# Gathered rows fetched whole, or cut in two at partition 32 or at partition 96, in turn by slot

## The chip, the core and the metric

The kernel runs on one core of one Trainium2 chip. The core has a matrix engine (TensorE, "PE"), a vector engine (VectorE, "DVE"), a scalar engine (ScalarE, "ACT"), a general one (GpSimd, "POOL") and an engine that issues transfers (SyncE, "SP"). Sixteen DMA engines move data between the chip's memory and the core's on-chip memory, which has 128 partitions. The metric is the time on the device, in microseconds, of one launch. Lower is better.

## The reference

One decoder layer over 256 tokens of width 2048, in float32. An input projection feeds a convolution branch and a sparse attention branch, an output projection and a layer norm follow, and then the part that matters here, a lookup of single-neuron experts:

```python
s = einsum('nhcd,hckd->nhck', q, sub_keys)            # 8 heads, 2 key sets of 128 keys
s1, i1 = top_k(s[:, :, 0], 16); s2, i2 = top_k(s[:, :, 1], 16)
cand_i = i1 * 128 + i2                                # 16 x 16 candidates a head
top_s, pos = top_k(s1 + s2, 16)
experts = take_along_axis(cand_i, pos)                # (256, 8, 16), of 16384
h = gelu(einsum('td,thed->the', x, u_tab[experts]))
y = einsum('the,thed->td', softmax(top_s) * h, v_tab[experts])
x = layer_norm(alpha * x + y)
```

Each token needs 128 rows of `u_tab` and the same 128 rows of `v_tab`, 8 KB each. The host puts a row of both next to each other, in one row of 16 KB of `uv_tab`.

## The kernel before

The first 430 us hold the projections, the convolution, the attention and the first layer norm. After them comes a loop over 256 slots. The tokens stand in the 128 partitions, in two tiles (i = 0 and 1) of 128 tokens; slot s stands for tile i and for the j-th expert (of 128) of every token in it, `(i, j) = ROW_OF[s]`. Slots 0 to 49 are of tile 0, then the tiles take turns.

For one slot, POOL issues a gather at L465: an indirect DMA that reads for each of the 128 partitions the row of `uv_tab` whose number stands in that partition of one column of `eid`, and writes it to one of the buffers `uv_row` (128 x 4096 float32, 2 MB; six of them, seven from slot 54 on, `PLACES` and `WIDER_AT`). VectorE then forms the dot product of the first half of each row with the token (`dot`, L1642), ScalarE makes the weight of it (`gelu`, L1158 and L1162) and a diagonal matrix (L1166), TensorE adds the weighted second half of the row to the sum in PSUM (`add_row`, L805), and VectorE adds its last 512 columns up to slot 239 (`add_last`, L1651). A gather into a buffer waits until both additions from the buffer are done (`y_done`, `y_last_done`). POOL takes the slots strictly in order.

Some rows are not fetched. VectorE counts which first keys are wanted most (`popularity`) and chooses sixteen (`choose`, at slot 37); the experts of these keys are computed for all tokens with dense products (`dense_part`, `v_dense`: their blocks come over SP's queue, 1 MB each). `mark` (L1577 to L1590) writes for each block of 16 experts their numbers into `eid`, and adds 16384 to those of the chosen keys: such a number is out of bounds, and the gather moves nothing for that partition. `mark` runs for the 13 of 16 blocks that are not in `BEFORE`, and its last instruction tells POOL by `picked` that the numbers are there. Every slot from 48 on has such blocks. The last two slots (`TAIL`) are gathered in halves, from `last_id`.

Two earlier transfers of POOL are used for comparison below. L425 reads `dist_row` from 16 partitions that lie 8 apart (0, 8, ..., 120) and writes 2 MB to `turned_rows` in the chip's memory, in pieces of 1 KB; L430 then reads these 2 MB back, in the same pieces, into all 128 partitions of `bias`.

`u_in[k]` is the semaphore of buffer k on which the gathers land, 16 for each gather; `dot` waits for 16 times the number of gathers into its buffer so far (`USES`).

Of the kernel before, what the change touches and what calls it, by code (L numbers as in the profile page):

```python
# [7 lines left out]
I32 = mybir.dt.int32  # L8
# [3 lines left out]
ALU = mybir.AluOpType  # L12
ACT = mybir.ActivationFunctionType
AX = mybir.AxisListType

P = 128
D = 2048
S = 256
TI = S // P
# [11 lines left out]
TOP = 16  # L31
SLOTS = PH * TOP
# [19 lines left out]
ALL = TI * SLOTS  # L52
WIDER_AT = 54
PLACE = [s % PLACES if s < WIDER_AT else (s - WIDER_AT + PLACES) % (PLACES + 1) for s in range(ALL)]
USES = [PLACE[:s + 1].count(PLACE[s]) for s in range(ALL)]
BEFORE_IT = [max((r for r in range(s) if PLACE[r] == PLACE[s]), default=-1) for s in range(ALL)]
TAIL = 2
# [9 lines left out]
SKIP = PK * PK  # L67
# [9 lines left out]
ROW_OF = ([(0, j) for j in range(ALONE)] + [((n + 1) % 2, n // 2 + (n % 2) * ALONE) for n in range(2 * (SLOTS - ALONE))]  # L77
          + [(1, j) for j in range(SLOTS - ALONE, SLOTS)])
# [6 lines left out]
BEFORE = [(0, 0), (0, 1), (0, 2)]  # L85
# [10 lines left out]
ASKED = [(0, 0), (0, 1), (1, 1), (1, 0)]  # L96
TURNED = ((0, 2, 1, 3), (0, 1, 2, 3))

def layer(nc, xT, x_tok, w_stream, w_kw, w_sub, conv_p, cln, bucket1h, rel_bias,
          b_out, ln1_col, ln_rows, uv_tab, dense_u, out):
    with ExitStack() as ctx:
        def sb(name, shape, dt=F32):
            return ctx.enter_context(nc.sbuf_tensor(name, shape, dt))

        def sem(name):
            return ctx.enter_context(nc.semaphore(name))
# [10 lines left out]
        def span(i):  # L119

            return slice(0, S) if i else slice(S, S + P)
# [9 lines left out]
        def put(name, where, shape, dt=F32, plus=0):  # L131
            return nc.alloc_sbuf_tensor_at(name, shape, dt, offset=arena0 + (spot[where] + plus) * KB)[:]
# [35 lines left out]
        row = [put(f"uv_row{k}", w, [P, 2 * D], plus=o) for k, (w, o) in enumerate(places)]  # L168
# [59 lines left out]
        val, idxf, posf = ([sb(f"{n}{c}", [P, TOP]) for c in range(2)] for n in ("val", "idxf", "posf"))  # L228
        of_dense = sb("of_dense", [P, TOP])
# [10 lines left out]
        eid = sb("eid", [P, TI * SLOTS], I32)  # L240

        dots = sb("dots", [P, TI * SLOTS])
        gel = sb("gel", [P, TI * SLOTS])
        weight = sb("weight", [P, TI * SLOTS])
        last_f = sb("last_f", [P, TAIL])
        last_id = sb("last_id", [P, 2, TAIL], I32)
# [11 lines left out]
        def at_early(name, shape, offset, dt=F32):  # L258
            return nc.alloc_sbuf_tensor_at(name, shape, dt, offset=early0 + offset)
# [11 lines left out]
        row_gate = at_early("row_gate", [P, TI, SLOTS], 6144)  # L271
# [48 lines left out]
        gate_sub, gate_exp, picked = sem("gate_sub"), sem("gate_exp"), sem("picked")  # L320
# [8 lines left out]
        gates_done, weight_done, y_last_done = sem("gates_done"), sem("weight_done"), sem("y_last_done")  # L329
# [4 lines left out]
        u_in = [sem(f"u_in{k}") for k in range(PLACES + 1)]  # L334
        v_in = [sem(f"v_in{k}") for k in range(TAIL)]
        dots_done, gelu_done, diag_done, y_done = (sem(n) for n in ("dots_done", "gelu_done", "diag_done", "y_done"))
# [66 lines left out]
        def _(pool):  # L403
# [31 lines left out]
            for c in range(2, CC):  # L435
                pool.wait_ge(conv_done, c + 1)
                pool.wait_ge(total_step, c - 1)
                last = pool.tensor_tensor(conv_total, conv_total, convT[:, c, :], ALU.add)
                last.then_inc(total_step if c < CC - 1 else conv_summed, 1)
            pool.wait_ge(squared, 1)  # L440
            for step, n in enumerate((CC // 2, CC // 4, CC // 8)):
                if step:
                    pool.wait_ge(sq_step, step)
                last = pool.tensor_tensor(sq[:, 0:n, :], sq[:, 0:n, :], sq[:, n:2 * n, :], ALU.add)
# [18 lines left out]
            def gather(dst, tab, ids, land):  # L463

                pool.indirect_dma_start(dst, None, tab, bass.IndirectOffsetOnAxis(ap=ids, axis=0),  # L465
                                        bounds_check=tab.shape[0] - 1, oob_is_err=False).then_inc(land, 16)

            halves = uv_tab.rearrange("n (a d) -> (n a) d", a=2)
            for s in range(ALL):
                k = PLACE[s]  # L470
                i, j = ROW_OF[s]
                if j % TOP == 0:
                    pool.wait_ge(picked, ORDER.index((i, j // TOP)) + 1)
                if k == 4 and s < PLACES:
                    pool.wait_ge(q_done, ASKED.index((1, 1)) + 1)
                if k == 5 and s < PLACES:
                    pool.wait_ge(x1_done, TI)
                if s == WIDER_AT:
                    pool.wait_ge(unit_scored, LATER)
                if BEFORE_IT[s] >= 0:  # L480
                    pool.wait_ge(y_done, BEFORE_IT[s] + 1)
                    pool.wait_ge(y_last_done, min(BEFORE_IT[s] + 1, JOIN_AT))
                if s < ALL - TAIL:
                    gather(row[k], uv_tab, eid[:, i * SLOTS + j:i * SLOTS + j + 1], u_in[k])
                else:
                    j = s - (ALL - TAIL)
                    gather(row[k][:, 0:D], halves, last_id[:, 0, j:j + 1], u_in[k])
# [454 lines left out]
        def _(act):  # L942
# [211 lines left out]
            def gelu(s):  # L1154

                i, j = ROW_OF[s]
                act.wait_ge(dots_done, s + 1)
                act.activation(gel[:, s:s + 1], dots[:, s:s + 1], ACT.Gelu).then_inc(gelu_done, 1)  # L1158
                if j % TOP == 0:
                    act.wait_ge(gates_done, ORDER.index((i, j // TOP)) + 1)  # L1160
                act.wait_ge(gelu_done, s + 1)
                act.activation(weight[:, s:s + 1], gel[:, s:s + 1], ACT.Identity, scale=row_gate[:, i, j:j + 1]).then_inc(weight_done, 1)  # L1162
                act.wait_ge(weight_done, s + 1)
                if BEFORE_IT[s] >= 0:
                    act.wait_ge(y_done, BEFORE_IT[s] + 1)
                act.activation(diag[PLACE[s]], ident[:, :], ACT.Identity, scale=weight[:, s:s + 1]).then_inc(diag_done, 1)  # L1166
# [40 lines left out]
            for s in range(3, ALL):  # L1207
# [5 lines left out]
                r, t = s // PACE + 1, s % PACE  # L1213
# [15 lines left out]
        def _(dve):  # L1229
            steps = [0]  # L1230

            def link(ins):

                steps[0] += 1
                ins.then_inc(dve_step, 1)
                dve.wait_ge(dve_step, steps[0])
# [51 lines left out]
            for u in range(CC):  # L1288
                lower(u + 2)
                dve.wait_ge(relu_done, 2 + u + 1)  # L1290
                for j in range(2):
                    for i in range(TI):
                        h = i * NH + 2 * u + j
                        last = dve.scalar_tensor_tensor(out=acc[i][:, :], in0=rel[u % 2][:, j, span(i)], scalar=widx[:, h:h + 1],
                                                        in1=acc[i][:, :], op0=ALU.mult, op1=ALU.add)
# [93 lines left out]
            for hp in range(CC):  # L1389
                for j in range(2):  # L1390
# [4 lines left out]
                    if hp == CC - 2 and j == 0:  # L1395
                        dve.wait_ge(mean_done, 1)
                        for c in range(CC):
                            last = dve.tensor_tensor(convT[:, c, :], convT[:, c, :], ps[7][:, 0:S], ALU.subtract)
# [38 lines left out]
            for n in range(3):  # L1437
# [3 lines left out]
                if n == 0:  # L1441
                    dve.wait_ge(row_in, 16)
                    dve.wait_ge(b_in, 16)
                    for i in range(TI):
                        last = dve.scalar_tensor_tensor(out=x1[:, i, :], in0=x1[:, i, :], scalar=ALPHA, in1=b_all,
                                                        op0=ALU.mult, op1=ALU.add)
# [11 lines left out]
                for i in range(TI):  # L1458
                    last = dve.bn_stats(stats[:, 4 * i + n, :], x1[:, i, n * 512:(n + 1) * 512])
# [65 lines left out]
            def across(t):  # L1525

                return t.rearrange("p (r o) -> p r o", o=1).to_broadcast(square)
# [49 lines left out]
            def mark(i, h):  # L1577

                q = i * PH + h
                first, second = (t[:, i, h * TOP:(h + 1) * TOP] for t in key_of)  # L1580
                dve.scalar_tensor_tensor(out=posf[0][:, :], in0=first, scalar=float(PK), in1=second, op0=ALU.mult, op1=ALU.add)
                link(dve.tensor_tensor(hit[0], across(first), down(dense_key[:, :]), ALU.is_equal))
                link(dve.tensor_reduce(of_dense[:, :], hit[0], AX.X, ALU.add))
                if q == TI * PH - 1:
                    link(dve.scalar_tensor_tensor(out=last_f[:, :], in0=of_dense[:, TOP - TAIL:TOP], scalar=float(SKIP),
                                                  in1=posf[0][:, TOP - TAIL:TOP], op0=ALU.mult, op1=ALU.add))
                    for a in range(2):
                        link(dve.tensor_scalar(last_id[:, a, :], last_f[:, :], 2.0, float(a), ALU.mult, ALU.add))
                dve.scalar_tensor_tensor(out=eid[:, q * TOP:(q + 1) * TOP], in0=of_dense[:, :], scalar=float(SKIP),
                                         in1=posf[0][:, :], op0=ALU.mult, op1=ALU.add).then_inc(picked, 1)  # L1590

            def divide(i, h):

# [40 lines left out]
            def dot(s):  # L1634

                k = PLACE[s]
                dve.wait_ge(u_in[k], 16 * USES[s])
                if s == PLACES:
                    dve.wait_ge(key_copied, len(ASKED))
                if s > PLACES:  # L1640
                    dve.wait_ge(dots_done, s)
                dve.tensor_tensor_reduce(row[k][:, 0:D] if s < PLACES else product, row[k][:, 0:D], x1[:, ROW_OF[s][0], :], 1.0, 0.0, ALU.mult, ALU.add,  # L1642
                                         dots[:, s:s + 1]).then_inc(dots_done, 1)
# [68 lines left out]
            for s in range(ALL - TAIL):  # L1712
# [7 lines left out]
                r, t = s // PACE + 1, s % PACE  # L1720
# [63 lines left out]
            for s in range(ALL - TAIL, ALL):  # L1784
                dve.wait_ge(weight_done, s + 1)
                dve.wait_ge(v_in[s - (ALL - TAIL)], 16)
                for n in range(TAIL_BANKS, 4):
                    last = dve.scalar_tensor_tensor(out=bank(1, n), in0=row[PLACE[s]][:, D + n * 512:D + (n + 1) * 512],
                                                    scalar=weight[:, s:s + 1], in1=bank(1, n), op0=ALU.mult, op1=ALU.add)
# [78 lines left out]
```

## Time and profile before

| | us |
|---|---|
| median of 3 runs | 1663.65 (1663.07 to 1663.74) |
| the profiled execution | 1665.44 |
| its span, from the first to the last instruction | 1663.6 |

| engine | busy us | share of the span |
|---|---|---|
| TensorE, matmul | 1545.1 | 93% |
| VectorE | 1342.8 | 81% |
| ScalarE | 496.2 | 30% |
| GpSimd | 483.5 | 29% |

The DMA engines moved 571.57 MB, 450.03 MB of it over the queue that POOL issues to (q0). A TensorE that is busy 93% is not at its peak for 93%: the profile counts a matmul as busy while it is in the pipeline. The span falls into stages, and a share over all of it says little about any of them. The rows below are therefore mostly of windows, in us from the start of the span. A DMA share is the mean busy share of the 16 DMA engines; a waiting time stands for an engine that is idle until something releases it.

### The profile page before, as it was taken

To read this page: it belongs to the slowest core of one execution; us is meant where nothing else is said; L and a number is where in the kernel's file an instruction comes from. 1 tells how busy PE (TensorE), PEld (TensorE's weight loads), DVE (VectorE), ACT (ScalarE), POOL (GpSimd) and SP (SyncE) were. 2 spreads that over 40 slices of the span, in tenths; PEclk is the share of its full clock that TensorE was granted. 3 is DMA by queue.
4 is the path that set the end of the run, shared out by engine and by line. 5 is a ranking of instruction groups with operands and counts; after the bars stand their busy time and mean duration, and the time that the engine had idled before them with its cause. 6 is when DMAs were issued, how large, how long until landed. Compare 5 with 4: busy or idle time off the path is not lost.

```text
span 1663.6 us, 18502 instructions
## 1 busy us (share of the span) xinstructions
PE 1545.1 (93%) x6332; PEld 993.6 (60%) x6332; DVE 1342.8 (81%) x2260; ACT 496.2 (30%) x1142; POOL 483.5 (29%) x293
## 2 busy tenths in 40 slices
PE   9999999999999888998899999899999999998896
PEld 8999899888765444555455555355555444433332
DVE  4689999766778787988899999899998766655577
ACT  5433344734222221233222222212222311111121
POOL 0100110100123223434444444444544322332231
PEclk9999999999999999999999999999999999999999
DMA  6664544474799999999999999999999999999994
GB/s 248 197 234 177 201 155 151 180 301 177 292 416 426 427 427 428 427 418 399 413 388 404 407 376 405 416 412 380 403 381 401 361 408 416 418 407 382 351 349 183
DMA packets 58669, 571.57 MB, mean 344 GB/s; under 512 B 12969, under 2 KB 13641, under 8 KB 16713
## 3 DMA queue, kind: packets, MB, share of 16 engines
q0 software_dynamic: 39328, 450.03, 66.4%
q1 hardware_dynamic: 18580, 120.22, 19.1%
q8 instruction: 47, 0.77, 0.2%
q14 instruction: 42, 0.34, 0.1%
q10 hardware_dynamic: 672, 0.21, 0.1%
HBM read 665.68 MB, written 4.19 MB: 403 GB/s over the span
## 4 chain that ended last, share of the span: by engine, by line
DMA 39%; PE 38%; DVE 13%; issue 6%; ACT 2%; POOL 1%; SPq 0%; POOLq 0%; DVEq 0%
DMA uv_row<-in_uv_tab,eid 37%; PE psum L805 10%; PE psum L500 6%; PE psum L502 6%; PE psum L501 6%; DVE scratch L1642 5%; PE psum L898 4%; POOL uv_row L465 1%; DMA w_raw<-in_w_stream 1%; PE psum L826 1%; DVE y_last L1651 1%; PE psum L746 1%; DVE first_key L1662 1%; PE psum L630 1%; DVE w_lo L1261 1%
## 5 line engine op out<-in xcount | busy, mean ns | idle before, releaser
L805 PE MATMUL psum<-uv_row,scratch 128*128 128x512 f32 x1560 | 742.0, 614 | 95.1 <-ACT scratch L1166 94.3
L1642 DVE CUSTOM_DVE_ANT_0 scratch<-uv_row,x 128x2048 bf16<-128x2048 f32 x250 | 572.5, 2290 | 206.0 <-DMA uv_row<-in_uv_tab,eid 205.0
L465 POOL DMA_INDIRECT uv_row<-in_uv_tab,eid x254 | 440.4, 1734 | 752.1 <-DVE y_last L1651 402.2
L805 PEld LDWEIGHTS psum<-uv_row,scratch 128*128 128x128 f32 x1560 | 289.8, 193 | 436.8 <-issue 282.2
L1158 ACT ACTIVATE gel<-dots 128x1 f32<-128x1 f32 x256 | 51.9, 203 | 820.9 <-DVE dots L1642 820.8
L500 PE MATMUL psum<-xT_hi,w_hi 128*128 128x256 f32 x640 | 183.8, 287 | 3.5 <-DVE w_lo L1261 2.9
L1651 DVE SCALAR_TENSOR_TENSOR y_last<-uv_row,weight,y_last 128x512 f32<-128x512 f32 x240 | 179.8, 749 | 3.3 <-ACT weight L1162 1.3
L502 PE MATMUL psum<-xT_hi,w_lo 128*128 128x256 f32 x640 | 181.7, 284 | 0.0
L501 PE MATMUL psum<-xT_lo,w_hi 128*128 128x256 f32 x640 | 181.7, 284 | 0.0
L1261 DVE TENSOR_TENSOR w_lo<-w_raw,w_hi 128x2048 fp32r<-128x2048 f32 x62 | 141.7, 2288 | 29.0 <-ACT w_hi L957 28.1
L957 ACT ACTIVATE w_hi<-w_raw 128x2048 fp32r<-128x2048 f32 x62 | 118.8, 1916 | 85.9 <-DMA w_raw<-in_w_stream 85.9
L500 PEld LDWEIGHTS psum<-xT_hi,w_hi 128*128 128x128 f32 x640 | 123.4, 193 | 7.4 <-issue 3.1
L501 PEld LDWEIGHTS psum<-xT_lo,w_hi 128*128 128x128 f32 x640 | 123.5, 193 | 0.1
L502 PEld LDWEIGHTS psum<-xT_hi,w_lo 128*128 128x128 f32 x640 | 123.4, 193 | 0.0
L858 PEld LDWEIGHTS psum<-x1T,dense_unit 128*128 128x128 f32 x512 | 97.4, 190 | 40.6 <-issue 30.7
L898 PE MATMUL psum<-dense_unit,scratch 128*128 128x512 f32 x256 | 121.0, 595 | 0.0
L858 PE MATMUL psum<-x1T,dense_unit 128*128 128x256 f32 x512 | 121.0, 379 | 0.0
L1166 ACT ACTIVATE scratch<-ident,weight 128x128 f32<-128x128 f32 x256 | 102.9, 402 | 8.4
L898 PEld LDWEIGHTS psum<-dense_unit,scratch 128*128 128x128 f32 x256 | 48.8, 192 | 63.4 <-issue 63.4
L1333 DVE SCALAR_TENSOR_TENSOR scratch<-glu_sb,conv_sb,scratch 128x256 f32<-128x256 f32 x203 | 82.7, 478 | 0.0
L886 PEld LDWEIGHTS psum<-scratch,first_key 128*128 128x128 f32 x512 | 65.6, 194 | 24.3 <-issue 24.3
L1162 ACT ACTIVATE weight<-gel,row_gate 128x1 f32<-128x1 f32 x256 | 75.6, 295 | 14.9 <-DVE gate L1630 5.3
(247 smaller groups left out, 1408.7 us busy)
## 6 DMA issues: line engine op xcount, KB each, us to landing
w_raw<-in_w_stream SPq DMA_DIRECT2D x63, 1024.0 KB, 4.8
dense_unit<-in_dense_u SPq DMA_DIRECT2D x16, 1024.0 KB, 11.1
dense_unit<-in_uv_tab SPq DMA_DIRECT2D x16, 1024.0 KB, 11.2
wq_first<-in_w_stream SPq DMA_DIRECT2D x8, 1024.0 KB, 11.4
wq_third<-in_w_stream SPq DMA_DIRECT2D x4, 1024.0 KB, 11.7
uv_row<-in_uv_tab,eid POOLq DMA_INDIRECT x254, 20.9
xT_raw<-in_xT SPq DMA_DIRECT2D x4, 512.0 KB, 5.5
turned_rows<-dist_row POOLq DMA_DIRECT2D x1, 2048.0 KB, 14.0
```

The lines of the kernel that those rows point to most:

```text
L465: pool.indirect_dma_start(dst, None, tab, bass.IndirectOffsetOnAxis(ap=ids, axis=0), bounds_check=tab.shape[0] - 1, oob_is_err=False).then ...
L500: pe.matmul(dst, a[0], b[0], start=first, stop=False)
L501: pe.matmul(dst, a[0], b[1], start=False, stop=False)
L502: return pe.matmul(dst, a[1], b[0], start=False, stop=last)
L805: last = pe.matmul(bank(i, n), diag[k], row[k][:, D + n * 512:D + (n + 1) * 512], start=False, stop=True, skip_group_check=True)
L858: last = pe.matmul(spare[v % 2][:, 0:S], w[:, c, :], x1T[:, c, :], start=c == 0, stop=c == KC - 1)
L898: last = pe.matmul(bank(i, n), mixed[:, v, i * P:(i + 1) * P], dense_unit[v % 2][:, n * 512:(n + 1) * 512], start=v == 0 and n == PE_BANKS ...
L957: act.activation(w_hi[k], w_raw[k], ACT.Copy).then_inc(hi_done, 1)
L1166: act.activation(diag[PLACE[s]], ident[:, :], ACT.Identity, scale=weight[:, s:s + 1]).then_inc(diag_done, 1)
L1261: dve.tensor_tensor(w_lo[k], w_raw[k], w_hi[k].bitcast(F32), ALU.subtract).then_inc(lo_dve, 1)
L1642: dve.tensor_tensor_reduce(row[k][:, 0:D] if s < PLACES else product, row[k][:, 0:D], x1[:, ROW_OF[s][0], :], 1.0, 0.0, ALU.mult, ALU.add, ...
L1651: dve.scalar_tensor_tensor(out=y_last[:, i, :], in0=row[k][:, D + 3 * 512:2 * D], scalar=weight[:, s:s + 1], in1=y_last[:, i, :], op0=ALU. ...
```

## The change

Every gather from slot 49 to slot 253 whose experts are of a block outside `BEFORE` now comes in one of three ways, by its place in the block of 16 (`CUT`): whole; or as two gathers, of partitions 0-31 and 32-127; or as two, of partitions 0-95 and 96-127. Of the 254 whole-row gathers, 65 are cut at 32, 64 at 96, and 125 stay as they are; POOL issues 129 more. The second gather takes its row numbers from `eid_moved`, in which `mark` puts the numbers of the upper partitions at partition 0 and up, with four copies for each block. `dot` waits for the landings of all gathers of its slot (`LANDED`). To make room for `eid_moved`, the buffer `gel` is gone, and the GELU is written over its argument in `dots`.

```diff
+CUTS = (P, 32, 96)
+CUT = [CUTS[ROW_OF[s][1] % TOP % len(CUTS)] if (ROW_OF[s][0], ROW_OF[s][1] // TOP) not in BEFORE and s < ALL - TAIL else P
+       for s in range(ALL)]
+LANDED = [sum(1 + (CUT[r] < P) for r in range(s + 1) if PLACE[r] == PLACE[s]) for s in range(ALL)]
...
-        gel = sb("gel", [P, TI * SLOTS])
+        eid_moved = sb("eid_moved", [P, TI * SLOTS], I32)
...
                 if s < ALL - TAIL:
-                    gather(row[k], uv_tab, eid[:, i * SLOTS + j:i * SLOTS + j + 1], u_in[k])
+                    ids, cut = i * SLOTS + j, CUT[s]
+                    gather(row[k][0:cut], uv_tab, eid[0:cut, ids:ids + 1], u_in[k])
+                    if cut < P:
+                        gather(row[k][cut:P], uv_tab, eid_moved[0:P - cut, ids:ids + 1], u_in[k])
...
-                act.activation(gel[:, s:s + 1], dots[:, s:s + 1], ACT.Gelu).then_inc(gelu_done, 1)
+                act.activation(dots[:, s:s + 1], dots[:, s:s + 1], ACT.Gelu).then_inc(gelu_done, 1)
...
-                dve.scalar_tensor_tensor(out=eid[:, q * TOP:(q + 1) * TOP], in0=of_dense[:, :], scalar=float(SKIP),
-                                         in1=posf[0][:, :], op0=ALU.mult, op1=ALU.add).then_inc(picked, 1)
+                link(dve.scalar_tensor_tensor(out=eid[:, q * TOP:(q + 1) * TOP], in0=of_dense[:, :], scalar=float(SKIP),
+                                              in1=posf[0][:, :], op0=ALU.mult, op1=ALU.add))
+                for n, cut in enumerate(CUTS):
+                    at_cut = slice(q * TOP + n, (q + 1) * TOP, len(CUTS))
+                    for p in range(cut, P, 32):
+                        last = dve.tensor_copy(eid_moved[p - cut:p - cut + 32, at_cut], eid[p:p + 32, at_cut])
+                last.then_inc(picked, 1)
...
-                dve.wait_ge(u_in[k], 16 * USES[s])
+                dve.wait_ge(u_in[k], 16 * LANDED[s])
```

On POOL, the gathers of slots 47 to 53 before (the number in `uv_row1` and so on is the buffer, the shape is partitions x elements):

```order
L465 DMA uv_row5_89<-in_uv_tab,eid 128x4096
L465 DMA uv_row0_84<-in_uv_tab,eid 128x4096
L465 DMA uv_row1_85<-in_uv_tab,eid 128x4096
L465 DMA uv_row2_86<-in_uv_tab,eid 128x4096
L465 DMA uv_row3_87<-in_uv_tab,eid 128x4096
L465 DMA uv_row4_88<-in_uv_tab,eid 128x4096
L465 DMA uv_row5_89<-in_uv_tab,eid 128x4096
```

and the same slots now:

```order
L470 DMA uv_row5_89<-in_uv_tab,eid 128x4096
L470 DMA uv_row0_84<-in_uv_tab,eid 128x4096
L470 DMA uv_row1_85<-in_uv_tab,eid 32x4096
L470 DMA uv_row1_85<-in_uv_tab,eid_moved 96x4096
L470 DMA uv_row2_86<-in_uv_tab,eid 128x4096
L470 DMA uv_row3_87<-in_uv_tab,eid 96x4096
L470 DMA uv_row3_87<-in_uv_tab,eid_moved 32x4096
L470 DMA uv_row4_88<-in_uv_tab,eid 32x4096
L470 DMA uv_row4_88<-in_uv_tab,eid_moved 96x4096
L470 DMA uv_row5_89<-in_uv_tab,eid 128x4096
```

Slots 49, 51 and 52 now have two gathers; no other instruction of POOL has moved. The waits for the buffer stand ahead of the first of the two.

On VectorE, the end of `mark` and the start of `divide` (which sets the gates of the same block) before:

```order
L1583 TENSOR_REDUCE of_dense<-scratch 128x16
L1589 SCALAR_TENSOR_TENSOR eid<-of_dense,posf 128x16
L1595 SCALAR_TENSOR_TENSOR row_gate<-of_dense,gate 128x16
```

and now:

```order
L1591 TENSOR_REDUCE of_dense<-scratch 128x16
L1597 SCALAR_TENSOR_TENSOR eid<-of_dense,posf 128x16
L1602 COPY eid_moved<-eid 32x5 x4
L1608 SCALAR_TENSOR_TENSOR row_gate<-of_dense,gate 128x16
```

Four small copies (32 partitions x 5 numbers each) have come in, and POOL is told only after the last of them. That happens 13 times. TensorE, ScalarE and SyncE have the same instructions in the same order as before.

## Rows read from the trace of the kernel before

**Rows 1.** The page, part 2: DMA in 40 slices of 41.6 us.
```profile
DMA  6664544474799999999999999999999999999994
GB/s 248 197 234 177 201 155 151 180 301 177 292 416 426 427 427 428 427 418 399 413 388 404 407 376 405 416 412 380 403 381 401 361 408 416 418 407 382 351 349 183
```
**Rows 2.** The page, part 4: the chain that ended last, by line.
```profile
DMA uv_row<-in_uv_tab,eid 37%; PE psum L805 10%; PE psum L500 6%; PE psum L502 6%; PE psum L501 6%; DVE scratch L1642 5%; PE psum L898 4%; POOL uv_row L465 1%; DMA w_raw<-in_w_stream 1%; PE psum L826 1%; DVE y_last L1651 1%; PE psum L746 1%; DVE first_key L1662 1%; PE psum L630 1%; DVE w_lo L1261 1%
```
**Rows 3.** Stretches: length, PE, PEld, DVE, ACT, POOL busy (count), PEclk, DMA share, GB/s.
```profile
72.00:75.00 3.00, 3.00 (x27) 3.00 (x27) 2.65 (x6) 1.82 (x1) 0.38 (x2) 1.00 1.00 370
75.00:80.00 5.00, 5.00 (x44) 5.00 (x44) 4.60 (x13) 1.38 (x2) 2.31 (x1) 1.00 0.98 191
88.00:90.00 2.00, 2.00 (x19) 2.00 (x18) 0.43 (x1) 1.47 (x1) 0.00 (x0) 1.00 1.04 360
480.00:700.00 220.00, 191.96 (x621) 114.77 (x620) 176.59 (x384) 56.81 (x160) 67.11 (x42) 0.98 1.01 427
722.00:1066.00 344.00, 314.25 (x958) 179.26 (x957) 311.36 (x647) 98.54 (x268) 153.52 (x77) 0.99 0.98 401
1066.00:1260.00 194.00, 177.66 (x726) 106.23 (x725) 182.65 (x195) 40.54 (x135) 87.40 (x45) 0.95 0.98 397
1270.00:1435.00 165.00, 163.72 (x394) 71.97 (x393) 111.97 (x115) 38.43 (x122) 54.08 (x38) 1.00 0.98 399
1435.00:1566.00 131.00, 120.49 (x267) 50.65 (x266) 77.02 (x78) 23.41 (x78) 37.09 (x27) 0.97 0.97 391
1566.00:1612.00 46.00, 42.24 (x96) 17.52 (x95) 32.60 (x34) 11.87 (x33) 14.43 (x11) 1.00 0.91 345
```
**Rows 4.** VectorE's waits for gathers, 722:1066, 1066:1260, 1435:1566, 1566:1612: us, times, longest.
```profile
DVE scratch L1642 <- DMA uv_row<-in_uv_tab,eid: 25.9, 19, 4.0
...
DVE scratch L1642 <- DMA uv_row<-in_uv_tab,eid: 10.6, 14, 1.8
...
DVE scratch L1642 <- DMA uv_row<-in_uv_tab,eid: 53.9, 25, 4.4
...
DVE scratch L1642 <- DMA uv_row<-in_uv_tab,eid: 14.4, 10, 2.4
```
**Rows 5.** The chain in order of time, 1566 to 1664 us: start, us, what.
```profile
1584.50 22.91 DMA uv_row<-in_uv_tab,eid
...
1618.81 22.25 DMA uv_row<-in_uv_tab,eid
1641.08 2.29 DVE scratch L1642
```
**Rows 6.** The stretch in which the last gathers are under way, columns as in rows 3.
```profile
1620.00:1641.00 21.00, 17.42 (x39) 6.81 (x38) 12.43 (x13) 4.50 (x15) 7.68 (x4) 1.00 0.86 337
```
**Rows 7.** POOL's queue in 722:1066, 1066:1260, 1270:1435, 1435:1566: packets, MB, share.
```profile
q0 software_dynamic: 10682, 120.98, 86.2%
...
q0 software_dynamic: 6658, 76.96, 97.8%
...
q0 software_dynamic: 5342, 58.43, 87.1%
...
q0 software_dynamic: 3938, 43.83, 82.4%
```
**Rows 8.** Line L425: its one instruction, duration ns min/median/max and its start.
```profile
L425 POOL DMA_DIRECT2D turned_rows<-dist_row x1: 1263/1263/1263, 67.6 to 67.6; - x1
```
**Rows 9.** The tile `eid`: duration ns min/median/max; the last line is the gathers' landing.
```profile
L465 POOL DMA_INDIRECT uv_row<-in_uv_tab,eid x254: 987/1740/3047, 431.8 to 1618.8; - x127
L1589 DVE SCALAR_TENSOR_TENSOR eid<-of_dense,posf x13: 174/174/177, 664.2 to 1041.0; 128x16 int32<-128x16 f32 x13
...
DMA to landing us min/median/max: 8.7/20.9/28.7
```
**Rows 10.** A small copy of VectorE, 600 to 1066 us: busy us, mean ns, idle before.
```profile
L1617 DVE COPY gsum<-gate 128x1 f32<-128x1 f32 x12 | 1.8, 147 | 0.0
```
**Rows 11.** The page, part 5: the gathers' issues, busy us, mean ns, idle before.
```profile
L465 POOL DMA_INDIRECT uv_row<-in_uv_tab,eid x254 | 440.4, 1734 | 752.1 <-DVE y_last L1651 402.2
```

More of the change, by code:

```diff
@@ L1161, in gelu @@
                 act.wait_ge(gelu_done, s + 1)
-                act.activation(weight[:, s:s + 1], gel[:, s:s + 1], ACT.Identity, scale=row_gate[:, i, j:j + 1]).then_inc(weight_done, 1)
+                act.activation(weight[:, s:s + 1], dots[:, s:s + 1], ACT.Identity, scale=row_gate[:, i, j:j + 1]).then_inc(weight_done, 1)
                 act.wait_ge(weight_done, s + 1)
```

## The prediction, made before the changed kernel ran

> **What bounds the kernel now.** I read the slices first, then the chain, then windows by stage, then who waits in each. The slices show the DMA engines at 9 tenths from slice 12 on, where the gathers begin, and 427 GB/s at best, then 350 to 420 [rows 1]. The chain that ended last has 37% of the span in gathers, more than any other line [rows 2]. By stage [rows 3]: from 480 to 700 us, before any row is left out, 427 GB/s at a DMA share of 1.01, so 427 is what full engines move. From 722 to 1066 it is 401 GB/s at 0.98 with VectorE busy 311 of 344 us; from 1066 to 1260 397 GB/s, VectorE 183 of 194; from 1270 to 1435 TensorE is busy 163.7 of 165 us and bounds; from 1435 to 1566 nothing computes all the time (TensorE 120 of 131, VectorE 77) and the DMA moves 391. VectorE waits for gathers 25.9, 10.6, 53.9 and 14.4 us in the four windows where TensorE does not bound [rows 4], 105 us together.
>
> Two rows say that the sixteen DMA engines are not loaded alike late in the loop. From 1566 to 1612 us VectorE waits for gathers while the engines are busy only 0.91 of the time and move 345 GB/s [rows 3, 4]. The last whole gather is issued at 1618.81 and takes 22.25 us [rows 5], about 6 times what its bytes need, in a stretch with a DMA share of 0.86 [rows 6]. A gather has landed when its slowest engine is done. Rows of chosen keys are left out, and whoever serves the tokens with few such rows has more to fetch.
>
> **How much a gather moves.** POOL's queue moved 120.98, 76.96, 58.43 and 43.83 MB in the four windows from 722 to 1566 us [rows 7], in which 77, 45, 38 and 27 gathers were issued [rows 3]: 300.2 / 187 = 1.605 MB each. At 427 GB/s that is 3.76 us. The slots come every 344/77 = 4.47, 194/45 = 4.31, 165/38 = 4.34 and 131/27 = 4.85 us, part of which is SP's own loads. So the DMA has next to no slack, and whatever slows a cut gather shows in the end.
>
> **The change, part by part.** POOL: 129 more issues. An issue lasts 0.99 to 3.05 us, 1.74 in the median [rows 9], so 128 to 393 us on an engine that sat idle for 752 us before its gathers [rows 11]. Even two issues of 1.74 fit into a slot of 4.3, so POOL does not bound. The second part of a slot starts one issue later, 1.0 to 3.0 us. Hidden as long as the DMA engines have a backlog, which a landing time of 20.9 us [rows 9] for 3.76 us of bytes shows; if they had none, a buffer comes round every 6 or 7 slots and the price would be 129 x 1.74 / 7 = 32 us. I take 0.
>
> VectorE: 13 x 4 = 52 copies of 32 x 5 numbers. The nearest copy takes 147 ns [rows 10], the instruction ahead of them 174 [rows 9]: 7.6 to 9.0 us in all, in a stage where VectorE idles 33 us of 344 [rows 3]. Below: 0, behind waits for gathers; above: 9. They also delay `picked` by 0.6 us a block, for which POOL waits only at a block's first slot. I take 3 where the DMA does not bound, and 0 where it does. ScalarE: same instructions, another column; nothing. TensorE and SP: nothing moves.
>
> The DMA: the bytes stay. What changes is which sixteenth of a gather each engine carries, and that a part of it goes to 32 partitions alone. For the price of that there is one row. The transfer of L425 [rows 8] has one side in 16 partitions, and from 75 to 80 us it moved 191 GB/s at a DMA share of 0.98, alone on the queues; the same 1 KB pieces going into all 128 partitions moved 360 [rows 3]. Full engines and half the rate: they got in each other's way at something. Against this reading: in its first 3 us, 72 to 75, the rate was 370 [rows 3], so part of it may be the memory on the other side, which gathers do not write.
>
> Bounds for a cut slot of 1.605 MB. The 32 partitions carry a quarter, 0.401 MB: 0.94 us at 427 GB/s, 2.10 us at 191. The 96 carry 1.204 MB: 2.82 us at 427, 6.30 us at 191. For the 32 I take 191, since that row had few partitions too (16). For the 96 I take three quarters of 427, 320 GB/s, 3.76 us: an estimate, near the fast end, since most partitions are reached. Added per cut slot: (2.10 - 0.94) + (3.76 - 2.82) = 2.10 us. For 129 slots: +271 us. Less what the DMA had spare where TensorE bounds, 1270 to 1435: 165 us at 399 against 427 GB/s, 11 us. Sum: +260 us, with both ends at 0 (all at 427) and 129 x (1.16 + 3.48) = +599 us (all at 191).
>
> [...] No row here shows a gather into 32 partitions. [...]
>
> **The profiled execution.** It took 1665.44 us against a median of 1663.65. 1665.4 + 260 = 1925, less 1.8: 1924 us.
>
> **Rival 1: it evens the engines out.** If only the engines count, a division by 2 and by 6 neighbours mixes with the old one. From the reference's inputs I counted the rows that are fetched, per slot, for groups of eight partitions (four neighbours and the four 32 further; my assumption on the old division). Heaviest group before and heaviest engine after: slots 49-124 6.69 and 6.58, 125-179 7.02 and 6.76, 180-239 6.77 and 6.60, 240-253 7.21 and 6.36, with means of 6.20, 6.34, 6.06 and 5.90. A row costs an engine 16 x 16384 B / 427 GB/s = 0.614 us. Gain: 76 x 0.11 x 0.614 + 55 x 0.26 x 0.614 + 60 x 0.17 x 0.614 + 14 x 0.85 x 0.614 = 5.1 + 8.8 + 6.3 + 7.3 = 27 us, less 4 where TensorE bounds and 3 for VectorE: 20 us, so 1644, between 1630 and 1658. For it: the unequal load above is real [rows 3, 5, 6], and the 105 us of waits [rows 4] leave room. Against it: 75 to 80 us [rows 3], and that heaviest groups fall by 2 to 4% only, but for the last 14 slots.
>
> **Rival 2: nothing moves.** If an engine is tied to partitions however a transfer is cut, the load stays as it is and nothing collides. Then the copies and the later second issues remain: 1664 + 3 = 1667 us, between 1661 and 1680. For it: all gathers before looked alike, so the trace does not tell. Against it: nothing but that 16 of 16 engines were busy for a transfer from 16 partitions [rows 3].
>
> **Chances.** Slower by the collisions 0.60, 1924 us, its own range 1700 to 2200: the low end if only the 32 partitions suffer for part of the time, the high end if the engines, once out of step, meet at every cut gather. Rival 1 0.24, rival 2 0.16. A change under 0.2% (3.3 us) cannot be told from none. Faster: 0.24 of rival 1 and 0.01 of rival 2, 0.25. Same: 0.09, all rival 2. Slower: 0.60 + 0.06 = 0.66. The range runs from 1640, which takes in half of rival 1 and all of rival 2, to 2100, which leaves out about 0.08 of the main case.
>
> **What would show it.** Right: from 722 us on the DMA share stays at 0.95 or above while GB/s falls to about 300, VectorE's waits for gathers grow from 105 to over 300 us, the median landing of a cut gather rises over 25 us, and 480 to 700 us (uncut slots) is unchanged. Rival 1: GB/s rises above 401 in 722 to 1066, and the last gather's 22.25 us shrink by 5 or more. Rival 2: all windows alike, 129 issues more. The forecast is wrong if the rate in the cut stages stays above 380 GB/s; the failing step would then be the 191 GB/s taken over from L425.

## The result, and the profile after

The changed kernel takes 2546.05 us (median of 4 runs, 2531.72 to 2561.68) against 1663.36 (4 runs of the kernel before on the same chip, 1659.34 to 1663.74): a ratio of 1.5308 [1.5258, 1.5357], 883 us slower. The forecast was 1924, with a range of 1640 to 2100. The direction was right, and so was that full DMA engines would move less; the loss was more than three times the 260 us of the forecast, and that comes from two steps of its sum, not from one number.

The slices of the page of the changed kernel, part 2, 63.9 us each, to be held against [rows 1]. The cut gathers begin in the eleventh, at 695 us.

```profile
PE   9999999988865555656665466666675666567665
DVE  5899867877944344454544344544443333333345
DMA  6754475999999999999999999999999999999996
GB/s 221 238 182 165 148 281 221 428 427 427 409 202 181 194 195 218 198 200 203 207 201 183 187 204 216 204 183 180 195 202 209 204 213 238 200 203 207 198 197 174
```

The DMA engines stay at 9 tenths, and what they move falls to a half from one slice to the next. The bytes are the same (571.59 MB, of which q0 450.04). By stretch, with the columns of [rows 3]:

```profile
480.00:700.00 220.00, 189.31 (x605) 112.60 (x604) 177.53 (x396) 55.72 (x155) 69.31 (x41) 0.97 1.01 424
722.00:1066.00 344.00, 202.73 (x474) 104.25 (x473) 152.29 (x335) 45.11 (x126) 62.22 (x57) 0.81 1.00 197
1066.00:1500.00 434.00, 257.03 (x585) 128.95 (x584) 195.45 (x387) 58.44 (x164) 86.02 (x77) 0.78 1.00 198
1500.00:2000.00 500.00, 332.63 (x893) 167.26 (x891) 224.51 (x235) 57.36 (x185) 108.24 (x96) 0.76 0.98 199
2000.00:2400.00 400.00, 255.47 (x450) 100.88 (x450) 135.70 (x138) 40.59 (x136) 72.33 (x73) 0.85 0.99 209
```

480 to 700 us, where no slot is cut but the last one, is as it was. After that the rate is 197 to 209 GB/s at a share of 0.98 to 1.00: no engine is idle, but each is twice as long on a byte. POOL's queue alone, 722 to 1066 us, against the first line of [rows 7]:

```profile
q0 software_dynamic: 5614, 59.60, 88.8%
```

Before, 0.862 x 344 us x 16 engines for 120.98 MB are 39.2 engine-us a MB; now 0.888 x 344 x 16 for 59.60 MB are 82.0. VectorE's waits for gathers, in us, times, longest, over the whole run, first of the kernel before (the 105 us of [rows 4] are of four windows), then of the changed one:

```profile
DVE scratch L1642 <- DMA uv_row<-in_uv_tab,eid: 205.0, 138, 4.4
```
```profile
DVE scratch L1655 <- DMA uv_row<-in_uv_tab,eid_moved: 694.5, 126, 12.9
DVE scratch L1655 <- DMA uv_row<-in_uv_tab,eid: 395.5, 98, 9.5
```

So VectorE waits 1090 us for gathers against 205, and in nearly every slot (224 waits), not in the 129 cut ones alone. The tile `eid_moved`, POOL's and VectorE's instructions as in [rows 9], and the landing times of the page's part 6:

```profile
L470 POOL DMA_INDIRECT uv_row<-in_uv_tab,eid_moved x129: 904/953/2995, 695.1 to 2494.8; - x129
L1602 DVE COPY eid_moved<-eid x52: 158/163/271, 661.5 to 1381.2; 32x5 int32<-32x5 int32 x52
```
```profile
dense_unit<-in_dense_u SPq DMA_DIRECT2D x16, 1024.0 KB, 22.3
...
uv_row<-in_uv_tab,eid POOLq DMA_INDIRECT x254, 23.5
uv_row<-in_uv_tab,eid_moved POOLq DMA_INDIRECT x129, 47.9
```

The second parts of slots take 47.9 us to land. SP's loads suffer as well: the same transfer of `dense_unit` landed after 11.1 us before. TensorE's granted clock is 0.76 to 0.85 of full speed on average in the four later windows, since part of the time it is half of it (0.50 from 910 to 915 us). TensorE has gaps there (busy 203 of 344 us from 722 to 1066 us), VectorE's waits are for gathers, and in the probes below, where TensorE does nothing, the clock is 0.50; so we read the clock as a consequence. No run here changes it alone.

### The profile page after: what moved, and what is told of

Its sections match the earlier page's. It is cut to its first block and busy times, and to the rows that moved or that the text cites. A ratio compares the mean times of both kernels' runs of the same rounds, so it can differ in the third digit from the quotient of the medians.

```text
span 2557.3 us, 18812 instructions
## 1 busy us (share of the span) xinstructions
PE 1820.8 (71%) x6332; PEld 1081.6 (42%) x6332; DVE 1357.2 (53%) x2312; ACT 494.0 (19%) x1142; POOL 483.8 (19%) x422
## 2 busy tenths in 40 slices
DMA packets 60735, 571.59 MB, mean 224 GB/s; under 512 B 15033, under 2 KB 15705, under 8 KB 18777
## 3 DMA queue, kind: packets, MB, share of 16 engines
q0 software_dynamic: 41392, 450.04, 75.5%
## 5 line engine op out<-in xcount | busy, mean ns | idle before, releaser
L813 PE MATMUL psum<-uv_row,scratch 128*128 128x512 f32 x1560 | 997.2, 791 | 711.4 <-ACT scratch L1174 711.3
L813 PEld LDWEIGHTS psum<-uv_row,scratch 128*128 128x128 f32 x1560 | 365.8, 248 | 1207.5 <-ACT scratch L1174 821.5
L470 POOL DMA_INDIRECT uv_row<-in_uv_tab,eid x254 | 310.1, 1221 | 1586.4 <-DVE y_last L1664 1304.3
L1166 ACT ACTIVATE dots<-dots 128x1 f32<-128x1 f32 x256 | 51.9, 203 | 1744.9 <-DVE dots L1655 1744.9
L470 POOL DMA_INDIRECT uv_row<-in_uv_tab,eid_moved x129 | 133.8, 1038 | 40.7 <-issue 40.7
## 6 DMA issues: line engine op xcount, KB each, us to landing
dense_unit<-in_dense_u SPq DMA_DIRECT2D x16, 1024.0 KB, 22.3
uv_row<-in_uv_tab,eid_moved POOLq DMA_INDIRECT x129, 47.9
```

The lines of the kernel that those rows point to most:

```text
L813: last = pe.matmul(bank(i, n), diag[k], row[k][:, D + n * 512:D + (n + 1) * 512], start=False, stop=True, skip_group_check=True)
```

## The experiments

Ratios are against runs of the kernel before on the same chip, which took 1663.68 us (e1 to e4), 1664.59 (e5 to e8) and 1668.47 (e9, e10). In the three probes, gathers stand behind the end of the kernel before, where nothing else runs. Their issue on POOL took 1 us (33.72 us for 34 of them, e5). The windows shown are up to 2.4 us shorter than the time from the first to the last packet of a group, which gives the times in the text of e1. Each probe ran once, e4, e6 and e10 twice, e7 and e8 four times, e2 and e3 ten times. A cut gather of a probe takes its row numbers from the first partitions of `eid`, not from `eid_moved`; the bytes of a train change by under 1% by that.

**e1_probe: gathers by destination.** Twelve groups of six slots, each into six buffers, with a wait between groups. `(lo, hi)` are the partitions of one gather.

```diff
+WHOLE, AT_32, AT_96 = [(0, P)], [(0, 32), (32, P)], [(0, 96), (96, P)]
+PROBES = [([WHOLE], 6), ([[(0, 64)]], 6), ([[(32, 96)]], 6), ([[(64, P)]], 6), ([[(0, 32)]], 6), ([[(0, 16)]], 6),
+          ([[(32, P)]], 6), ([[(0, 96)]], 6), ([WHOLE, AT_32, AT_96], 6), ([AT_32], 6), ([AT_96], 6), ([AT_32, WHOLE, WHOLE, WHOLE, WHOLE, WHOLE], 6)]
...
+                for t in range(times):
+                    for lo, hi in parts[t % len(parts)]:
+                        gather(row[t % PLACES][lo:hi], uv_tab, eid[0:hi - lo, t:t + 1], probe)
```

> The kernel before with gathers added behind its end, twelve groups of them, each group issued back to back into the six row buffers and waited for before the next; only the stretches behind about 1664 us count. [...] Theory B (a cut gather is served by fewer engines): 64 rows take the same time wherever they go, 30 us at a DMA share near 0.5. Theory C (a cut costs by the number of transfers): 64 rows take 15 us in all three places, and only the groups with two gathers a slot are slow.

Measured, one line for each group in this order:

```profile
1664.00:1692.00 28.00, 0.00 (x0) 0.00 (x0) 0.00 (x0) 0.00 (x0) 2.97 (x3) 0.50 0.99 425
1696.00:1725.00 29.00, 0.00 (x0) 0.00 (x0) 0.00 (x0) 0.00 (x0) 3.72 (x4) 0.50 1.00 208
1730.00:1745.00 15.00, 0.00 (x0) 0.00 (x0) 0.00 (x0) 0.00 (x0) 3.64 (x4) 0.50 0.96 400
1749.00:1778.00 29.00, 0.00 (x0) 0.00 (x0) 0.00 (x0) 0.00 (x0) 3.89 (x5) 0.50 1.01 210
1783.00:1798.00 15.00, 0.00 (x0) 0.00 (x0) 0.00 (x0) 0.00 (x0) 3.63 (x4) 0.50 0.94 197
1802.00:1815.00 13.00, 0.00 (x0) 0.00 (x0) 0.00 (x0) 0.00 (x0) 3.56 (x4) 0.50 0.94 102
1820.00:1859.00 39.00, 0.00 (x0) 0.00 (x0) 0.00 (x0) 0.00 (x0) 3.77 (x4) 0.50 0.99 236
1863.00:1903.00 40.00, 0.00 (x0) 0.00 (x0) 0.00 (x0) 0.00 (x0) 3.98 (x5) 0.50 1.00 227
1908.00:1956.00 48.00, 0.00 (x0) 0.00 (x0) 0.00 (x0) 0.00 (x0) 8.00 (x9) 0.50 0.99 259
1961.00:2014.00 53.00, 0.00 (x0) 0.00 (x0) 0.00 (x0) 0.00 (x0) 9.32 (x10) 0.50 1.00 231
2019.00:2072.00 53.00, 0.00 (x0) 0.00 (x0) 0.00 (x0) 0.00 (x0) 9.58 (x11) 0.50 1.01 233
2077.00:2111.00 34.00, 0.00 (x0) 0.00 (x0) 0.00 (x0) 0.00 (x0) 4.97 (x5) 0.50 0.97 362
```

The last column tells it. 64 partitions move at 208 or 210 GB/s as 0-63 or 64-127, and at 400 as 32-95; 32 partitions (0-31) move at 197, 16 at 102. It is which partitions are written, not how many rows there are. 0-63 gets hardly more than 0-31 (208 against 197), and 32-95, with the same number of rows, twice as much; our reading is that 0-31 and 32-63 share something that 64-127 has once more. Theory B had the same 30 us for 64 rows wherever they go, at a share near 0.5, and theory C 15 us wherever they go; 64 rows took 16.8 us in 32-95 and 30.9 and 30.8 in the two other places, at a share of 0.96 to 1.01, so neither holds. The parts of 96 partitions, at 236 and 227 GB/s, take in partitions of both halves and still get hardly more than 0-63: six of them took 40 to 42 us. Six cut slots took 55 us. A slot of the changed kernel's mix took 49.4 / 6 = 8.2 us (whole ones 30.4 / 6 = 5.1); its 12.58 MB in 49.4 us are 255 GB/s.

**e2_uncut: the change without its cuts.** Copies, `eid_moved`, GELU in place; each slot in one gather.

```diff
-                    gather(row[k][0:cut], uv_tab, eid[0:cut, ids:ids + 1], u_in[k])
-                    if cut < P:
-                        gather(row[k][cut:P], uv_tab, eid_moved[0:P - cut, ids:ids + 1], u_in[k])
+                    gather(row[k], uv_tab, eid[:, ids:ids + 1], u_in[k])
```

> The changed kernel with its copies to eid_moved and its GELU in place, but every gather whole, as before. [...] If the copies on VectorE or the GELU in place cost something, it is this run that shows it; over 1700 us would clear the gathers.

Measured: 1664.04 us, a ratio of 1.0004 [0.9990, 1.0017]. The 52 copies and the waits cost nothing that can be measured.

**e3_columns: as many gathers, in all partitions.** The 129 slots come as two gathers of 128 partitions and 8 KB a row, the u half and the v half.

```diff
-                    gather(row[k][0:cut], uv_tab, eid[0:cut, ids:ids + 1], u_in[k])
...
+                        gather(row[k][:, 0:D], u_tab, eid[:, ids:ids + 1], u_in[k])
+                        gather(row[k][:, D:2 * D], v_tab, eid[:, ids:ids + 1], u_in[k])
```

> The same 129 slots in two gathers each, but both into all 128 partitions: first the 2048 columns of u, then the 2048 of v, from tables of their own. [...] Theory C (more transfers, two gathers of a slot on one semaphore, twice the packets): most of the 883 us stays, over 2200 us.

Measured: 1665.77 us, 1.0013 [1.0000, 1.0026]. 722 to 1066 us, where 123 gathers are issued in place of 77:

```profile
722.00:1066.00 344.00, 311.21 (x949) 179.08 (x948) 315.71 (x678) 98.39 (x268) 221.45 (x123) 0.98 0.99 399
```

So the number of gathers, POOL's issues and the later second issue are no cause. With e2, what is left is the splitting by partitions.

**e4_at64: two of three slots cut in the middle.**

```diff
-CUTS = (P, 32, 96)
+CUTS = (P, 64, 64)
```

> Two of three slots cut at 64, one whole. [...] Theory that only the unequal parts (32 and 96) hurt: under 1800 us.

Measured: 2507.15 us, 1.5071 [1.5024, 1.5119].

```profile
722.00:1100.00 378.00, 228.32 (x549) 118.43 (x549) 176.50 (x383) 53.56 (x148) 73.30 (x68) 0.84 1.00 208
```

Equal halves do nearly as badly as the change (844 us against 883): the loss does not need unequal parts of 32 and 96 partitions.

**e5_long_probe: trains of 36 slots, six in flight.** Whole and mixed, with all rows and with a column of `eid` of which some are left out; then twelve slots one at a time; then two halves.

```diff
+PROBES = [([WHOLE], 36, ALL_IN, 0), ([WHOLE, AT_32, AT_96], 36, ALL_IN, 0), ([WHOLE], 36, LEFT_OUT, 0), ([WHOLE, AT_32, AT_96], 36, LEFT_OUT, 0),
+          ([WHOLE], 12, ALL_IN, 1), ([WHOLE, AT_32, AT_96], 12, ALL_IN, 1), ([[(0, 64), (64, P)]], 36, ALL_IN, 0)]
```

> The kernel before with seven trains of gathers behind its end; a buffer is refilled as soon as its last gather has landed, six slots in flight. [...] 36 slots in two halves at 64: about 204 GB/s, as in the first probe. Theory D (something else in the loop, other engines' traffic or the stage, makes the 200): the long mix stays at 255 GB/s or more.

Measured, in this order:

```profile
1664.00:1840.00 176.00, 0.00 (x0) 0.00 (x0) 0.00 (x0) 0.00 (x0) 33.72 (x34) 0.50 1.00 428
1844.00:2169.00 325.00, 0.00 (x0) 0.00 (x0) 0.00 (x0) 0.00 (x0) 55.29 (x59) 0.50 0.97 232
2173.00:2331.00 158.00, 0.00 (x0) 0.00 (x0) 0.00 (x0) 0.00 (x0) 33.73 (x34) 0.50 0.87 351
2335.00:2644.00 309.00, 0.00 (x0) 0.00 (x0) 0.00 (x0) 0.00 (x0) 55.15 (x58) 0.50 0.91 181
2648.00:2750.00 102.00, 0.00 (x0) 0.00 (x0) 0.00 (x0) 0.00 (x0) 10.92 (x11) 0.50 0.64 244
2754.00:2891.00 137.00, 0.00 (x0) 0.00 (x0) 0.00 (x0) 0.00 (x0) 18.01 (x19) 0.50 0.67 182
2895.00:3246.00 351.00, 0.00 (x0) 0.00 (x0) 0.00 (x0) 0.00 (x0) 65.85 (x70) 0.50 1.01 215
```

The long mix, with all rows, moved 232 GB/s, less than the 255 of the six-slot group in e1, so theory D does not hold. The mix costs 325 / 36 - 176 / 36 = 4.1 us a slot, which is 6.2 for each cut slot; with rows left out (309 - 158) / 36 x 1.5 = 6.3. One at a time, so that every slot starts on drained engines, it is (137 - 102) / 12 x 1.5 = 4.4. About 2 us of a cut are thus paid only in a running train; that the engines have fallen out of step there is our reading. One at a time, a whole slot took 102 / 12 = 8.5 us and a mixed one 137 / 12 = 11.4. Whole gathers with rows left out move 351 GB/s at a share of 0.87, against 428 at 1.00 with all rows. Most of what is missing is at the end of the train: 389 GB/s at 0.96 up to 2309 us, then 115 at 0.29 for 22 us, when some engines still have rows to fetch and the others have none.

**e6_only_96 and e10_only_32: one of the two ways alone.**

```diff
-CUTS = (P, 32, 96)
+CUTS = (P, P, 96)
```

(`(P, 32, P)` in e10.)

> Only the 64 cuts at 96 are left, the 65 slots that were cut at 32 are whole. If a cut costs by itself, from the first probe (cut at 96 54.8 us for six slots against 30.4 whole, 4.1 us a cut with all rows, 3.1 with three quarters): 64 x 3.1 to 4.1 = 200 to 260 us, 1865 to 1925. If each cut also slows the whole gathers behind it, because the engines have lost step, in proportion to the cuts: 883 x 64 / 129 = 440 us, about 2100.

> Only the 65 cuts at 32 are left. The 64 cuts at 96 alone cost 9.7 us each; if a cut at 32 is the same, 65 x 9.7 = 630 us, 2295. If the side matters (the large part second instead of first), it differs by more than 100 us from 2288.

Measured: 2287.82 us, 1.3741 [1.3658, 1.3823], for 64 cuts at 96, 9.7 us each; 2307.58 us, 1.3844 [1.3748, 1.3939], for 65 cuts at 32, 9.8 us each. 722 to 1100 us of both:

```profile
722.00:1100.00 378.00, 248.83 (x620) 130.66 (x621) 199.47 (x427) 61.24 (x168) 85.19 (x64) 0.85 0.99 234
```
```profile
722.00:1100.00 378.00, 248.43 (x635) 131.02 (x634) 204.41 (x442) 62.10 (x170) 71.85 (x64) 0.88 0.99 235
```

Both ways are equally dear, both are dearer than the 2100 us of the higher of e6's two expectations, and half the cuts bring 71 and 72% of the loss. The cost is not one price times the number of cut slots. At least some of it must fall on whole gathers: cut slots are a third of the slots here, and a third of the bytes at 233 GB/s (six cut slots, e1) with the rest at the old 401 would make 323, not 234. e9 shows it directly.

**e7_sparse: 13 cuts at 32, one a block.**

```diff
-CUT = [CUTS[ROW_OF[s][1] % TOP % len(CUTS)] if ... else P
+CUT = [CUTS[1] if ROW_OF[s][1] % TOP == 1 and ... else P
```

> Thirteen slots are cut, at 32, one in each block of 16. First probe: one cut slot and five whole ones take 35.3 us against 30.4, 4.9 us. Additive: 13 x 3.2 to 4.9 = 42 to 64 us, 1705 to 1727, less what TensorE's stage hides. If one cut keeps the engines out of step for the following slots: over 1740. If a lone cut is absorbed by the backlog: under 1680.

Measured: 1783.98 us, 1.0723 [1.0699, 1.0746]: 119 us, 9.2 for each cut, about twice the additive expectation and in the range given for engines that stay out of step.

```profile
722.00:1100.00 378.00, 320.48 (x946) 183.29 (x945) 309.32 (x680) 91.88 (x254) 142.90 (x75) 0.95 0.98 353
```

Five percent of the slots are cut, and the rate over the stretch is down to 353 GB/s (401 from 722 to 1066 us before). The loss lies around the cuts. Second parts are issued at 870.6 and 887.4 us and at 1032.8 and 1042.9 us; the rate is 410 GB/s from 800 to 870 us, 242 from 870 to 910, 391 from 910 to 1030 and 253 from 1030 to 1080.

**e8_even_load: is the unequal load real?** The kernel before, whole gathers; which experts are left out is not the choice by keys but a fixed pattern, a fourth of all rows, the same number in each neighbourhood of partitions. It fetches no row for those experts and still weighs them, so its output is not the reference's.

```diff
-                dve.scalar_tensor_tensor(out=eid[:, q * TOP:(q + 1) * TOP], in0=of_dense[:, :], scalar=float(SKIP),
+                dve.scalar_tensor_tensor(out=eid[:, q * TOP:(q + 1) * TOP], in0=even[:, :], scalar=float(SKIP),
```

> Whole gathers, no eid_moved, but the rows left out are no longer those of the chosen keys: in each of the 13 blocks a fourth of the rows by a fixed pattern ((partition + place) divisible by 4), so that each group of eight partitions fetches 6 of 8 rows in every slot (6.18 on average before, up to 7.2 in the heaviest group of a stage). The gates still follow the chosen keys, so the output is not the reference's. It shows what evening out the engines could have brought at most: rival 1 said 27 us of row counts; with 0.18 rows fewer on average another 0.18 x 0.614 x 206 = 23 us at most. If the uneven load is what holds the loop back: 1600 to 1640 us. If VectorE's and TensorE's order is next at once: 1645 to 1660.

Measured: 1594.96 us, 0.9581 [0.9568, 0.9595]: 70 us less, and less than the 1600 to 1640 expected.

```profile
722.00:1066.00 344.00, 328.95 (x1042) 192.12 (x1041) 333.62 (x670) 103.39 (x286) 167.21 (x82) 1.00 1.00 420
```
```profile
1400.00:1530.00 130.00, 130.00 (x304) 57.53 (x304) 84.94 (x87) 26.07 (x87) 36.10 (x30) 1.00 1.01 425
```

420 GB/s in place of 401, and from 1400 to 1530 us TensorE is busy 130.0 of 130 us where it was 124.4 before. Not all of the 70 us is evenness: this kernel also fetches less, 440.45 MB over POOL's queue against 450.03, which at 427 GB/s is 22 us. Some 47 us are left for the even load, an estimate. So the premise of rival 1 holds, and an even load would be worth more than the 20 us it was given.

**e9_place_probe: one cut in twelve, and three places.** Trains as in e5.

```diff
+ONE_IN_12 = [AT_32] + [WHOLE] * 11
+PROBES = [([WHOLE], 36, ALL_IN, 0), (ONE_IN_12, 36, ALL_IN, 0), ([WHOLE], 36, LEFT_OUT, 0), (ONE_IN_12, 36, LEFT_OUT, 0),
+          ([[(32, 96)]], 36, ALL_IN, 0), ([[(16, 80)]], 36, ALL_IN, 0), ([[(0, 64)]], 36, ALL_IN, 0)]
```

> Again seven trains of 36 slots behind the kernel before, six in flight. Whole slots 4.92 us with all rows and 4.42 with a block that leaves rows out, as in the second probe. With one slot in twelve cut at 32 (three cuts): if a lone cut costs by itself, 3 x 4.3 = 13 us more than whole, with all rows and with rows left out; if the 9.2 us a cut of the sparse kernel arise in the DMA, because an engine that has lost step meets others for long, 3 x 9 = 27 us, above all with rows left out; if they arise in the loop (VectorE and TensorE kept waiting in order), 13 us in both. 64 rows into 32-95: 2.5 us a slot, 427 GB/s. Into 0-63: 4.9 us. [...]

Measured, in this order:

```profile
1664.00:1841.00 177.00, 0.00 (x0) 0.00 (x0) 0.00 (x0) 0.00 (x0) 33.97 (x35) 0.50 1.00 426
1845.00:2037.00 192.00, 0.00 (x0) 0.00 (x0) 0.00 (x0) 0.00 (x0) 36.59 (x38) 0.50 0.99 392
2041.00:2199.00 158.00, 0.00 (x0) 0.00 (x0) 0.00 (x0) 0.00 (x0) 33.62 (x34) 0.50 0.87 351
2203.00:2389.00 186.00, 0.00 (x0) 0.00 (x0) 0.00 (x0) 0.00 (x0) 36.45 (x37) 0.50 0.89 298
2393.00:2483.00 90.00, 0.00 (x0) 0.00 (x0) 0.00 (x0) 0.00 (x0) 31.90 (x34) 0.50 0.99 417
2487.00:2669.00 182.00, 0.00 (x0) 0.00 (x0) 0.00 (x0) 0.00 (x0) 31.87 (x34) 0.50 0.99 206
2673.00:2854.00 181.00, 0.00 (x0) 0.00 (x0) 0.00 (x0) 0.00 (x0) 31.93 (x35) 0.50 1.00 207
```

With all rows fetched, three cuts cost (192 - 177) / 3 = 5 us each; with rows left out, (186 - 158) / 3 = 9.3 each. The latter is the price in e7 (9.2), which a sum of single cuts had missed.

Parts of the two trains with one cut in twelve show where the price is paid. First with all rows, around the second cut slot and behind it, then the same with rows left out:

```profile
1907.00:1923.00 16.00, 0.00 (x0) 0.00 (x0) 0.00 (x0) 0.00 (x0) 1.98 (x2) 0.50 1.01 297
1925.00:1965.00 40.00, 0.00 (x0) 0.00 (x0) 0.00 (x0) 0.00 (x0) 9.56 (x10) 0.50 1.01 430
```
```profile
2247.00:2275.00 28.00, 0.00 (x0) 0.00 (x0) 0.00 (x0) 0.00 (x0) 2.96 (x3) 0.50 0.99 224
2275.00:2299.00 24.00, 0.00 (x0) 0.00 (x0) 0.00 (x0) 0.00 (x0) 4.94 (x5) 0.50 0.97 389
```

With all rows, 16 us are slow, 4.8 MB or about two slots of 2.1 MB, and the whole gathers behind them run at 430 GB/s again. With rows left out, 28 us run at 224 GB/s. That is 6.3 MB, four slots of 1.55 MB (the train's 351 GB/s x 158 us / 36), of which one is cut: three whole gathers run at half rate beside it. The third cut slot, with rows left out, has a like stretch (32 us at 242 GB/s from 2307 us). The first, which finds the engines drained, has only 8 us at 213, and then it is 408.

And 64 partitions: 32-95 run at 417 GB/s, 16-79 at 206, although they too take in partitions of both halves. If only some engines got in each other's way and the others waited for them, the share would be well below 1; it is 0.99. A row took 0.99 x 182 us x 16 engines / (36 x 64 rows) = 1.25 us of an engine's time on average, against 0.62 in 32-95. Had only half of the engines been slowed to this, the mean would be 0.94; and of the 2288 rows in this window 2273 took 1.1 to 1.3 us each. So all engines were slowed, and how is open. Which engine takes which rows of a part is not shown by any run.

## Why the prediction was wrong

**The bound and the bytes** were right: the DMA engines are full, a slot still moves 1.6 MB, and what slows it shows in the end. Of the views that it named, four came as written for the main case: a share of 0.98 to 1.00, waits of 1090 us, the second parts' landing at 47.9 us, 480 to 700 us unchanged. The fifth did not: about 300 GB/s were forecast, 197 to 209 came.

**POOL and VectorE at 0** were right. e2 bounds the copies and waits at -1.7 to +2.8 us, e3 adds 129 issues for at most 4.3 us.

**The 32 partitions at 191 GB/s**, taken from L425 [rows 8], came out right, 197 in e1, but in part by luck. The reason given was that L425 had few partitions too, 16 of them; a gather into 16, 0-15, moved 102 GB/s (e1). It is which partitions, not how few.

**The 96 partitions at 320 GB/s** was the first step that failed. It rested on no row and was put near the fast end "since most partitions are reached". e1 gives 236 and 227. The one term put right, in the prediction's own form: 0.401 MB at 197 GB/s and 1.204 MB at 231.5 (the mean of the two) are 2.04 + 5.20 = 7.24 us against 3.76, +3.48 a cut slot, 129 x 3.48 - 11 = +438. That is 178 of the 623 us that were missed. Our reading, which the rates of e1 and e9 fit and the share of 16-79 (0.99, e9) does not wholly, is that engines slow each other when the partitions that they write at the same time share something, as 0-31 and 32-63 do.

**A price in cut slots only** was the second step, and the larger. It is in the shape of the sum, 129 x something. In e9 with rows left out, three whole gathers run at half rate with the second cut one; our reading is that a cut leaves the engines out of step and the next gather starts that way. The price is 4.4 us with one slot at a time (e5), in the mix's train 6.2 to 6.3 (e5), for one cut in twelve with rows left out 9.3 (e9), and in the kernel 6.8 (129 cuts), 9.7 and 9.8 (64 and 65) and 9.2 (13). The train with rows left out would give 129 x 6.3 = 813 of the 883 us. The prediction had named this ("if the engines, once out of step, meet at every cut gather") and put it at its own range's end of 2200, below even the +599 of all parts at 191 GB/s, which again counts cut slots only. That upper bound was none: it left out the whole slots and SP's loads, whose landing went from 11.1 to 22.3 us. A bound that holds slows all that moves: from 700 us to the end the kernel before moved 386 GB/s x 964 us = 372 MB, which at 191 GB/s take 984 us longer.

**Rival 1** had its premise right (e8) and its conclusion wrong: whatever the new division evened out, the collisions it brought cost 883 us. Its 27 us rest on groups of four neighbours and the four 32 further, which were the author's assumption; no run shows which engine takes which rows, and e8, whose rows are even in every four neighbours, does not tell this grouping from another. **Rival 2** is refuted by the result and by e1: the gathers into 0-31 kept the 16 engines at a share of 0.94, though 96 of the 128 partitions had no row to fetch.

**Still open.** A cut costs 9.3 us with rows left out and 5 with all rows, and the slow stretch at the second cut is 28 us in place of 16 (e9). Why it is longer was not settled: that fewer rows let some engines run ahead into the next gather, so that they find no common step again, fits but is argued, not shown. Nor is it shown how all engines are slowed in 16-79 (206 GB/s at a share of 0.99), when in 32-95 none is (417 at 0.99). Nor are the last 70 us of the 883 placed; SP's slower loads are a candidate.

No version came out that computes the same and beats the kernel before. e8 shows what there is to win with an even load in every slot: some 47 us of its 70.

## What to carry to other kernels

Where the DMA bounds, do not split a transfer by partitions (883 us here for 129 gathers more); split it by columns, which cost nothing here (e3: at most 4.3 us for as many). If a part of the partitions must be written alone, measure that very range: 32-95 ran at 417 GB/s, 16-79 and 0-63 at 206 and 207 (e9). And where transfers follow each other without a gap, a disturbance is not priced by its own length (9.2 us a cut in e7, where a sum of single cuts gave 3.2 to 4.9): forecast the state that the queue runs in afterwards, with a bound that holds for the undisturbed transfers as well.

## What was not expected of the hardware

A DMA share of 1.00 says nothing about progress: the same engines at 1.00 moved 428 GB/s in whole gathers (e5), 227 into partitions 0-95 alone (e1) and 197 in the changed kernel. 13 cut gathers of 254 cost 7% of the kernel. The rate of a gather into 64 partitions depended on where they begin, by a factor of two (417 and 206 GB/s, e9), with the same rows and bytes and the engines at 0.99 both times. And a single cut gather slowed whole ones beside it, where rows were left out, for 28 us (e9).
